# A two-layer trunk with expert FFN: VectorE's order behind the router, scaling on GpSimd, a later scatter wait, another head order

## What is computed

```python
h = rmsnorm(x, mix_norm[layer]); z = h @ w_in[layer]          # 4392 columns
a = dsa_attention(q, k, v, qi, ki, wi)                        # indexer keeps 64 keys a row
p = pool_mixer(u, w_pool[layer], pool_scale[layer])
merged = sigmoid(ga) * (a @ w_attn_proj[layer]) + sigmoid(gp) * (p @ w_pool_proj[layer])
x = x + merged @ w_out[layer]
h2 = rmsnorm(x, ffn_norm[layer])
# layer 0: x += swiglu(h2, dense_w1, dense_w3, dense_w2), width 2816
# layer 1: x += sum over the top 2 of 8 experts of gate * swiglu(h2, w1[e], w3[e], w2[e]), width 3584
```

## Time and profile before

| | |
|---|---|
| median of 3 runs | 1515.8 us (1512.97 to 1518.07) |
| profiled execution, its own time | 1514.89 us |
| its span | 1513.1 us |
| mean granted TensorE clock | 0.996 |
| busy, share of the span: TensorE | 99% |
| VectorE, ScalarE, GpSimd | 81%, 68%, 1% |

### The profile page before, as it was taken

One profiled execution on the slowest core, in us unless ns is written; L12 is line 12 of the kernel. 1 busy time (PEld: TensorE's weight loads), 2 busy tenths in 40 slices (PEclk: granted clock), 3 DMA queues, 4 the chain that ended last, 5 costly groups with the idle time before them and its releaser, 6 DMA issues.

```text
span 1513.1 us, 21384 instructions
## 1 busy us (share of the span) xinstructions
PE 1491.1 (99%) x6985; PEld 1232.6 (81%) x6985; DVE 1224.5 (81%) x1170; ACT 1030.0 (68%) x1022; POOL 13.4 (1%) x17
## 2 busy tenths in 40 slices
PE   8999999999999989999999999999999999999998
PEld 6888888888888868888888888888888888888886
DVE  5884755445885769899899899989988988988988
ACT  6556544335656467788688778778878777877775
POOL 0000000000000010000000000000000000000001
PEclk9999999999999999999999999999999999999999
DMA  9883655357652489799999989989989989989997
GB/s 327 301 266 128 203 177 184 111 175 240 229 186 94 139 319 373 239 375 408 369 354 408 406 324 408 411 319 408 409 316 409 408 322 409 408 327 399 407 345 276
DMA packets 219748, 465.87 MB, mean 308 GB/s; under 512 B 14721, under 2 KB 39465, under 8 KB 219705
## 3 DMA queue, kind: packets, MB, share of 16 engines
q1 hardware_dynamic: 217984, 458.97, 82.7%
q0 software_dynamic: 1632, 6.33, 1.2%
q10 hardware_dynamic: 88, 0.02, 0.0%
HBM read 449.52 MB, written 15.73 MB: 307 GB/s over the span
## 4 chain that ended last, share of the span: by engine, by line
PE 92%; DMA 3%; DVE 1%; issue 1%; ACT 1%; SPq 1%; POOL 0%; DVEq 0%; ACTq 0%; POOLq 0%
PE bank L886 64%; PE bank L1246 18%; DMA w_raw<-in_moe_w 2%; PE bank L1202 2%; PE bank L865 1%; PE bank L867 1%; PE bank L866 1%; PE bank L951 1%; PE bank L896 1%; DMA x_by_slot<-x_scaled_rows,row_of_choice 1%; SPq L412 1%; DMA w_raw<-in_w_in 0%; PE bank L1185 0%; PE bank L935 0%; PE bank L1006 0%
## 5 line engine op out<-in xcount | busy, mean ns | idle before, releaser
L1285 DVE TENSOR_TENSOR w_lo<-w_raw,w_hi 128x2048 fp32r<-128x2048 f32 (+1 forms) x444 | 768.7, 1750 | 94.5 <-ACT w_hi L530 77.6
L530 ACT ACTIVATE w_hi<-w_raw 128x2048 fp32r<-128x2048 f32 (+1 forms) x444 | 656.6, 1490 | 208.0 <-PE bank L886 100.0
L886 PE MATMUL bank<-w_hi,hT_hi 128*128 128x512 f32 (+1 forms) x1424 | 389.2, 395 | 7.5 <-ACT hiddenM L802 4.5
L886 PE MATMUL bank<-w_hi,hT_lo 128*128 128x512 f32 (+1 forms) x1424 | 380.5, 389 | 0.7 <-DVE hT_lo L1300 0.7
L886 PE MATMUL bank<-w_lo,hT_hi 128*128 128x512 f32 (+1 forms) x1424 | 379.8, 389 | 0.0
L886 PEld LDWEIGHTS bank<-w_hi,hT_lo 128*128 128x128 f32 x1424 | 267.3, 189 | 57.2 <-DVE hT_lo L1300 1.2
L886 PEld LDWEIGHTS bank<-w_lo,hT_hi 128*128 128x128 f32 x1424 | 267.4, 189 | 55.7
L886 PEld LDWEIGHTS bank<-w_hi,hT_hi 128*128 128x128 f32 x1424 | 261.0, 189 | 61.3 <-issue 11.1
L524 ACT ACTIVATE w_hi<-w_raw 128x2048 fp32r<-128x2048 f32 (+2 forms) x100 | 169.8, 1700 | 162.2 <-PE bank L886 123.5
L1280 DVE TENSOR_TENSOR w_lo<-w_raw,w_hi 128x2048 fp32r<-128x2048 f32 (+2 forms) x100 | 201.4, 2019 | 94.6 <-ACT w_hi L524 93.8
L1246 PE MATMUL bank<-w_hi,hiddenM_hi 128*128 128x512 f32 x448 | 139.5, 392 | 0.0
(11 more groups left out here) (271 smaller groups left out, 823.1 us busy)
## 6 DMA issues: line engine op xcount, KB each, us to landing
...
```

The costliest lines, as they stand in the source:

```text
L530: act.activation(whi[:, m % SLOTS, 0:n], raw8[m % 8][:, 0:n], ACT.Copy).then_inc(s_hi, 1)
L886: ins = pe.matmul(dst[t], a[:, k0 + k, t * P:(t + 1) * P], b[:, k, :], start=start and part == 0 and k == 0, stop=stop and part == 2 and k ...
L1285: dve.tensor_tensor(wlo[:, m % SLOTS, 0:n], raw8[m % 8][:, 0:n], whi[:, m % SLOTS, 0:n], ALU.subtract).then_inc(s_lo, 1)
```

## The change

Nothing of what the kernel computes is changed but the arithmetic order of one root. In parts:

1. ScalarE waits for the scatter behind the SiLU of the third block of a job, not ahead of the first SiLU of job 0.
2. The rows are scaled by GpSimd (two multiplications of 128x1024) ahead of its scatters, not by ScalarE.
3. On VectorE the reciprocal root of the rows, and the gate difference, move from ahead of the job table to behind the low halves of the gathered rows. TensorE gathers mean square and square root of each slot (two columns) in place of the root, so that one Newton step on three columns serves rows and slots.
4. ScalarE loads the table of the exponential before it waits for the gate difference.
5. TensorE's six fillers ahead of job 0 go; the first two chunks of a job wait for the high halves of the gathered rows, and for the low halves only at the second group of products.
6. Head: the warm-up is plain products with the identity; the parameters are transposed after four transposes of x; ScalarE and VectorE do the first half of the transposed x before the split of chunk 0; the gains product stands behind chunk 3, its copy behind the index rows.

```diff
@@ gpsimd, after the pool weights (before L492) @@
+            pool.wait_ge(s_rs, 4)
+            for t in range(TT):
+                pool.tensor_scalar(xn[:, t, :], X[:, t, :], st3[:, 3, t:t + 1], None, ALU.mult).then_inc(s_xn, 1)
             pool.wait_ge(s_xz, (2 * NJ - E + 1) * 16)
@@ scalar @@
+            act.wait_ge(s_pcol, 1)
+            hT_hi(0, 0, (0, 1))
             split(0, chunk_words(0))
-            act.wait_ge(s_pcol, 1)
-            hT_hi(0, 0)
+            hT_hi(0, 0, (2, 3))
...
-            act.activation(st[:, 2, :], st[:, 1, :], ACT.Sqrt).then_inc(s_rms, 1)
+            act.activation(st3[:, 2, 0:TT], st3[:, 1, 0:TT], ACT.Sqrt).then_inc(s_rms, 1)
...
             gathered_hi(0)
-            act.wait_ge(s_rs, 4)
-            for t in range(TT):
-                act.activation(xn[:, t, :], X[:, t, :], ACT.Copy, scale=st[:, 3, t:t + 1]).then_inc(s_xn, 1)
             act.nop().then_inc(m_y, LEAD)
             act.nop().then_inc(s_ys, 16)
+            act.activation(silu0[:, 1:2], cst[:, C_ONE:C_ONE + 1], ACT.Exp)
             act.wait_ge(s_gd, 1)
...
                     split_m(m + 1, n, j8 + dyn)
-                    if first:
+                    silu_m(b, first)
+                    if p == 2:
                         act.wait_ge(s_xsc, 2 * TT * 16)
-                    silu_m(b, first)
@@ tensor @@
-                    if n == 1:
-                        pe.wait_ge(s_pcol, 2)
...
                 z_block(1, 1)
+                if l == 0:
+                    pe.wait_ge(s_cst2, 16)
+                    pe.wait_ge(s_gn, 4 * 16)
+                    pe.matmul(bank[2][:, 0:4 * HD], cst[0:1, C_ONE:C_ONE + P], nrow[:], start=True, stop=True).then_inc(s_prt, 1)
...
                 pe.wait_ge(s_idxs, 2 * (l + 1))
+                pe.wait_ge(s_pcol, 2)
                 dots(0)
...
-                pe.transpose(bank[7][:, 0:P], ident, ident)
+                pe.matmul(bank[7][:, 0:P], ident, ident, start=True, stop=True)
             pe.wait_ge(s_x[0], 16)
-            x_T(0, 0)
+            x_src = lambda kc, t: X[:, t, kc * P:kc * P + P]
+            transposes_hT(x_src, (0,))
             pe.wait_ge(s_par, 3 * 16)
             pe.transpose(bank[6][:, 0:40], prow[:], cst[0:40, C_ID:C_ID + 40]).then_inc(s_prt, 1)
+            transposes_hT(x_src, (1,))
...
-            layer(0, 0, first=gains)
+            layer(0, 0)
...
             gather(0)
-            pe.wait_ge(s_rs, 4)
+            pe.wait_ge(s_rms, 4)
             for t in range(TT):
-                ins = pe.matmul(bank[6][:, 16:17], selR[:, t, :].bitcast(F32), st[:, 3, t:t + 1], start=t == 0, stop=t == TT - 1)
+                ins = pe.matmul(bank[6][:, 16:18], selR[:, t, :].bitcast(F32), st3[:, 1:3, t:t + 1], start=t == 0, stop=t == TT - 1)
             ins.then_inc(s_r0, 1)
-            keep_busy(6, 0)
...
-                            if first and j == 0:
-                                pe.wait_ge(s_glo, i * 2 + h + 1)
-                            chunk(MOE0 + 2 * j + h, [bank[4 + j][:]], hehi, helo, 4 * h, 512, h == 0, h == 1, dyn, tiles=1)
+                            rows = (s_ghi, s_glo, i * 2 + (h + 1)) if first and j == 0 else None
+                            chunk(MOE0 + 2 * j + h, [bank[4 + j][:]], hehi, helo, 4 * h, 512, h == 0, h == 1, dyn, tiles=1,
+                                  rows=rows)
@@ vector @@
+                if l == 0:
+                    dve.wait_ge(s_prt, 2)
+                    dve.tensor_copy(gain[:].rearrange("p l j d -> p (l j d)"), bank[2][:, 0:4 * HD]).then_inc(s_pcol, 1)
+                    dve.wait_ge(s_pcol, 2)
                 for n in range(1, 5):
...
+            hT_lo(0, 0, (0, 1))
             split(0, chunk_words(0))
-            hT_lo(0, 0)
+            hT_lo(0, 0, (2, 3))
             split(1, chunk_words(1))
-            dve.wait_ge(s_prt, 2)
-            dve.tensor_copy(gain[:].rearrange("p l j d -> p (l j d)"), bank[7][:, 0:4 * HD]).then_inc(s_pcol, 1)
...
             dve.nop().then_inc(s_ms, 1)
-            dve.wait_ge(s_rms, 4)
-            rsqrt(st[:, 3, :], st[:, 2, :], st[:, 1, :], st[:, 0, :])
-            dve.nop().then_inc(s_rs, 1)
-            dve.tensor_tensor(pr[:, 0, :], pr[:, 0, :], st[:, 3, :], ALU.mult).then_inc(s_gd, 1)
...
             gathered_lo(0)
             dve.wait_ge(s_r0, 1)
-            dve.tensor_copy(rs[:], bank[6][:, 16:17]).then_inc(s_rsj, 1)
+            chain(dve.tensor_scalar(st3[:, 1:3, TT:TT + 1], bank[6][:, 16:18].rearrange("p (a o) -> p a o", o=1), EPS, None, ALU.max))
+            rsqrt(st3[:, 3, :], st3[:, 2, :], st3[:, 1, :], st3[:, 0, :])
+            dve.nop().then_inc(s_rs, 1)
+            dve.tensor_copy(rs[:], st3[:, 3, TT:TT + 1]).then_inc(s_rsj, 1)
+            dve.tensor_tensor(pr[:, 0, :], pr[:, 0, :], st3[:, 3, 0:TT], ALU.mult).then_inc(s_gd, 1)
```

15 lines of the change are left out of this document (6 added, 9 removed).

## The result

| | before | changed |
|---|---|---|
| median | 1515.34 us (5 runs, 1512.63 to 1518.07) | 1502.58 us (5 runs, 1500.76 to 1505.61) |
| ratio, 95% interval | | 0.9923 [0.9903, 0.9943] |
| profiled execution, its own time | 1514.89 us | 1505.61 us |
| its span, mean granted clock | 1513.1 us, 0.996 | 1503.8 us, 0.996 |

The kernel is faster by 12.8 us; 13.3 were forecast, and 1502.5 us. The five executions of the changed kernel are spread: 1500.76, 1500.88, 1502.58, 1505.20 and 1505.61, with mean granted clocks of 1.000, 1.000, 0.999, 0.996 and 0.996. The profiled one is the slowest of them, so its trace holds a gain of 9.3 us, and something that took 4 to 5 back. One execution of a later run (parts 1 and 6 alone) took 1716.15 us at a mean granted clock of 0.817 and is left out there.

What follows compares the result with a forecast made beforehand. TensorE, busy 1491.1 of 1513.1 us, was taken to bound the kernel, with losses where it idles or is slow. 5.7 + 2.2 + 5.4 = 13.3 us, from the median 1515.8, gave 1502.5 us; range 1498.5 to 1509.

Steps and rivals of the forecast that it cites:

- Scatter wait, 5.7 forecast: Start of job 0: moving ScalarE's wait to the third block gains 5.7 us, 4 idle and the rest lower clock; bounds 2.5, 5.9.
- the slack of VectorE's product: First block of job 0: VectorE's product done at 561.0, wanted by TensorE at 562.5, slack 1.5 us, so nothing lost.
- Job table first, 2.2 forecast: Ahead of job 0: VectorE's earlier job table and TensorE's shorter path start the job at 546.0, not 548.19; 2.2 us gained.
- Head, 5.4 forecast: Kernel start: reordered work without a break brings index transposes to 29.2 from 34.66; 5.4 us gained, bounds 2.8 and 6.1.
- Scaling on GpSimd, 4.6 us at cost zero: Ahead of the scatters: GpSimd's two multiplications take 4.6 us, bounds 2.23 and 9.2, covered by blocks 0 to 2.
- The first rival: Job 0: GpSimd and VectorE hinder each other, subtractions stretched by 4.6 us, TensorE stalls 3.1 us: 1505.6; chance 0.13.
- The cover: Blocks 0 to 2 of job 0 hide GpSimd's scaling; rows land 7 us before ScalarE's wait, 12 before TensorE would notice.
- The point where it becomes slower than before: Third block of job 0: late scatter makes the kernel slower than before once GpSimd's pair takes 30 us; this rival's chance 0.03.
- Dropping the fillers: TensorE ahead of job 0: removing six fillers, 1.4 us, costs nothing while the clock stays at its upper level.
- a fall of the clock at the head: Rival at the kernel's start: the clock falls at 14 us all the same, head gives 2.8 us: 1505.1; chance 0.12.
- the signs that the prediction had named as wrong: Multiplications over 9 us, subtractions above 2.28, TensorE waiting for VectorE in block 1, clock 0.5 after 14, index transpose awaiting VectorE.
- Warm-up products worth nothing: Kernel start: transposes already raise the clock, so making the eight warm-ups plain products is worth nothing in the sum.

Runs made afterwards that it cites:

- parts 1 and 6 alone: Kernel before with only the scatter wait moved behind the third block's SiLU and the new head order with product warm-up: 1505.65 us, ratio 0.9935.
- fillers in the router: Changed kernel with five more filler products of TensorE in and behind the router: 1503.0 us, ratio 0.9932; its profiled execution took 1501.0 us.
- scaling on ScalarE: Changed kernel with the rows scaled by ScalarE behind the gate's exponential instead of by GpSimd: 1501.4 us, ratio 0.9911.

## Why the prediction was right

The median, the sum and its range held; point by point:

- **Scatter wait, 5.7 forecast.** Measured alone 5.7 by the medians. No idle of TensorE in block 0, as the slack of VectorE's product promised: L1720 starts at 557.37 and is wanted at 561.09. With fillers in the router, where no low clock delays TensorE, it is still busy for all of the 14 us from 547 to 561.
- **Job table first, 2.2 forecast.** In the trace with scaling on ScalarE, without a low clock at the gather, the job starts at 540.75; less the 5.3 us of the head that is 2.1 earlier than 548.19. In the changed kernel's own trace only 0.4 of it shows, since the gather ran at the lower clock and ended late, and the times of the run with parts 1 and 6 alone leave it between 0 and 3.1.
- **Head, 5.4 forecast.** 5.4 in the trace, 5.3 with this part alone, 3.9 to 4.6 in that run's times.
- **Scaling on GpSimd, 4.6 us at cost zero.** Mis-sized: it took 5.97, within the bounds (2.23 and 9.2). The first rival's mechanism is there, VectorE's subtraction 3.13 us for 2.28, but at 0.85 us and not 4.6, and so within the slack. The Trainium skill ("GPSIMD Engine Reference", Specifications) names the shared SBUF interfaces as contended where VectorE reads two SBUF inputs; the two subtractions, 3.13 beside GpSimd and 2.28 without, agree. The prediction's "about twice slower" is said in that page of the Trainium skill, under Engine selection, of operations with two inputs, and those with one are called roughly line-rate. This multiplication has one tensor input and took 2.99 us on GpSimd and 1.14 on ScalarE, 2.6 times as long; no run has it on VectorE. Cost zero holds as far as times tell: the quickest executions with the scaling on ScalarE are no quicker. The cover is 11 to 14 us deep (17 to 20 allowed, 6 used). The point where it becomes slower than before was put at 30 us of multiplications; 32.4 us were 3.5 us slower.
- **Dropping the fillers.** "Costs nothing as long as the clock stays at its upper level". The clock did not stay up: it fell in both profiled executions of the changed kernel and, by their times and mean clocks (0.995 to 0.996), in four more of its ten. This is what the prediction lacked: it placed a fall of the clock at the head, where there was none, and gave none to the gather, where one of 10.2 us cost 4. Dropping the fillers is not its cause by what was measured: it came with them in place too (parts 1 and 6 alone). Two of the signs that the prediction had named as wrong are there, a subtraction above 2.28 us and a clock of 0.5 after 14 us; the first cost nothing, the second was not where the prediction had looked.
- **Warm-up products worth nothing.** 0.33 us at the index transposes, below what the medians tell apart. The reason given was too strong. The trace of before showed that transposes raise the clock; three executions with transposes as warm-up reached the upper level at 10.7 (and fell again at 14.1), 12.4 and 21.9, while with products it came between 5.7 and 8.5 in each of eleven. The Trainium skill ("TensorE: Matmul & The Clock Gate", Part 4: PE-mode transpose) says that a transpose doesn't count as busy time "the same way"; the first three traces speak partly for it (late) and partly against transposes not counting at all, as the prediction had read it (10.7, with nothing but transposes and the parameter product ahead of it). The warm-up of products is also twice as long, 3.78 us for 1.97, which these runs don't separate from its kind.

The forecast of 1502.5 was made of 13.3 us at a full clock. The executions at a mean clock of 1.000 gave 14.4 to 14.6 (1515.34 less 1500.88 and 1500.76), those at 0.995 to 0.997 gave 9.7 to 10.9, and the median of the first five, 1502.58 at 0.999, fell between the two, on the predicted value. Over the ten executions of both runs of the changed kernel the median is 1504.6, 2 us above the forecast: the mechanisms of the wait and the head were right, the worth of the router's part is shown by positions in traces only, and the hit to a tenth of a microsecond is luck.
